# Hymba decoder step: the memory projection interleaved with the two norms around it

## The reference, cut to what matters

```
mk, mv = mem @ w_xk, mem @ w_xv                     # memory keys and values, both are outputs
h = h + rms_norm(merged @ w_out, n_mix_post)        # output projection, its norm, the residual
xn = rms_norm(h, n_x_pre)                           # norm ahead of the cross-attention
q = xn @ w_xq                                       # query projection
def rms_norm(x, g): return x * rsqrt(mean(x * x, -1) + 1e-6) * g
```

## Time and profile before

| | us |
|---|---|
| median of 3 runs | 1958.95 (1956.95 to 1961.89) |
| profiled execution | 1959.56 |
| its span | 1958.0 |
| TensorE busy in it | 1809.5 (92%) |
| VectorE, ScalarE, GpSimd busy | 949.1, 500.0, 117.1 |

### The profile page before, as it was taken

How to read it: one execution, slowest core, us unless ns; L and a number is a source line. 1 busy time by engine, 2 the same in 40 slices (tenths; PEclk the granted TensorE clock), 3 DMA queues, 4 the chain that set the end, 5 groups by cost and what they waited for, 6 DMA issues and landing times.

```text
span 1958.0 us, 32059 instructions
## 1 busy us (share of the span) xinstructions
PE 1809.5 (92%) x12999; PEld 1653.0 (84%) x12999; DVE 949.1 (48%) x1145; ACT 500.0 (26%) x862; POOL 117.1 (6%) x145
## 2 busy tenths in 40 slices
PE   7999989989989968998999699999999999999993
PEld 6999976555568957896789579999999999999982
DVE  6328888776655286422342583333233332233445
ACT  6212125666464112203331231110001000000122
POOL 2100020001320010001100110000000000000000
PEclk9999999999999989998999899999999999999995
DMA  5512137657883114114311121111112111111113
GB/s 168 147 56 76 54 122 216 200 165 213 305 260 132 43 65 172 65 43 151 121 52 43 43 108 45 43 43 44 43 43 58 49 43 44 43 43 37 49 55 122
DMA packets 136958, 187.28 MB, mean 96 GB/s; under 512 B 7705, under 2 KB 99035, under 8 KB 136344
## 3 DMA queue, kind: packets, MB, share of 16 engines
q1 hardware_dynamic: 122670, 121.47, 20.4%
q0 software_dynamic: 14192, 64.53, 9.3%
q10 hardware_dynamic: 2, 0.00, 0.0%
HBM read 165.65 MB, written 20.74 MB: 95 GB/s over the span
## 4 chain that ended last, share of the span: by engine, by line
PE 84%; DVE 6%; ACT 6%; issue 3%; DMA 0%; SPq 0%; DVEq 0%; POOLq 0%; ACTq 0%; POOL 0%
PE PS L1712 20%; PE PS L1713 20%; PE PS L1714 20%; PE PS L1702 7%; PE PS L1919 2%; PE PS L1941 2%; PE PS L1965 2%; PE PS L1840 2%; PE PS L2210 2%; ACT KTS L729 1%; PE PS L2002 1%; PE PS L1727 1%; PE PS L2231 1%; DVE Y L1232 1%; PE PS L1728 1%
## 5 line engine op out<-in xcount | busy, mean ns | idle before, releaser
L1712 PE MATMUL PS<-XH,WH 128*128 128x352 f32 x1968 | 635.6, 323 | 0.0
L1713 PE MATMUL PS<-XL,WH 128*128 128x352 f32 x1968 | 630.8, 321 | 0.0
L1714 PE MATMUL PS<-XH,WL 128*128 128x352 f32 x1968 | 630.5, 320 | 0.0
L1132 DVE CAST WH<-RAW 128x1024 fp32r<-128x1024 f32 x126 | 95.3, 757 | 690.2 <-PE PS L1714 667.3
L1713 PEld LDWEIGHTS PS<-XL,WH 128*128 128x128 f32 x1968 | 369.8, 188 | 0.0
L1712 PEld LDWEIGHTS PS<-XH,WH 128*128 128x128 f32 x1968 | 369.2, 188 | 0.0
L1714 PEld LDWEIGHTS PS<-XH,WL 128*128 128x128 f32 x1968 | 368.9, 187 | 0.0
L1273 DVE SCALAR_TENSOR_TENSOR CY<-GP,DW,CY 128x1024 f32<-128x1024 f32 x124 | 158.5, 1278 | 1.0 <-DVE CY L1276 1.0
L1134 DVE TENSOR_TENSOR WL<-RAW,WH 128x1024 fp32r<-128x1024 f32 x126 | 156.5, 1242 | 4.3
L1712 PE MATMUL PS<-HH,WH 128*128 128x352 f32 x462 | 149.0, 323 | 0.0
L1713 PE MATMUL PS<-HL,WH 128*128 128x352 f32 x462 | 148.1, 321 | 0.0
(11 more groups left out here) (339 smaller groups left out, 2326.0 us busy)
## 6 DMA issues: line engine op xcount, KB each, us to landing
PG<-in_cache_k SPq DMA_DIRECT2D x128, 256.0 KB, 3.0
PG<-in_cache_v SPq DMA_DIRECT2D x64, 256.0 KB, 4.2
PG<-in_cache_v POOLq DMA_DIRECT2D x64, 256.0 KB, 4.4
RAW<-in_w_gate SPq DMA_DIRECT2D x22, 512.0 KB, 4.0
RAW<-in_w_up SPq DMA_DIRECT2D x22, 512.0 KB, 5.1
RAW<-in_w_in SPq DMA_DIRECT2D x20, 512.0 KB, 6.4
h_spill<-H POOLq DMA_DIRECT2D x2, 4224.0 KB, 12.2
H<-h_spill POOLq DMA_DIRECT2D x2, 4224.0 KB, 13.5
```

The source lines that it names most:

```text
L1132: dve.tensor_copy(WH[v % 2][:, :, :], raw).then_inc(hi_done, 1)
L1712: pe.matmul(out, WH[u][:, k, :], xh[:, k, cols], start=(k == 0), stop=False)
L1713: pe.matmul(out, WH[u][:, k, :], xl[:, k, cols], start=False, stop=False)
L1714: mm = pe.matmul(out, WL[u][:, k, :], xh[:, k, cols], start=False, stop=(k == kt - 1))
```

## The change

- The transposes of the memory move in between output tiles 3 to 6, two channel tiles after each. MH and ML move to another place in memory, since the output projection still reads the old one. The memory's load is issued ahead of H's.
- The roots are taken "in columns": the sum over channels of 88 tokens is one matmul with the tokens as the weights and one column of ones moving, so 12 such matmuls leave 1056 sums in 88 partitions by 12 columns (`token_sums`). Root and reciprocal work on those 12 columns. Four matmuls a chunk spread them again over all partitions (`spread`). Both norms do so; the second one's sums and spread stand inside the first two query tiles.
- The memory's high weight parts are copied by ScalarE (`high_at`), VectorE makes the low parts (`low_at`). Key tiles, sums, spread and the work of the norms alternate in a written-out order.
- A value tile takes the memory as weights and the 128 weight columns as the moving operand, twice, for the two halves of the memory tokens (`mem_value_tile`). The result has tokens on partitions, so values are not turned back.
- H gets Y added on VectorE for even k and on GpSimd for odd k; the squares of H, now in Y, are added up in TB by GpSimd, one of eight adds for each k.
- Stores and loads on GpSimd's queue wait for the new semaphores in their places.

The diff, cut (the same names with unchanged meaning left out):

```diff
@@ memory
-        MH = at("MH", [P, KT, NMEM], F32R, R1)
-        ML = at("ML", [P, KT, NMEM], F32R, R1 + 8192)
-        VMT = at("VMT", [P, KT, NMEM], F32, R1 + 16384)
-        KMTOK = at("KMTOK", [P, 2, D], F32, R1 + 24576)
+        MH = at("MH", [P, KT, NMEM], F32R, R2B + 16384)
+        ML = at("ML", [P, KT, NMEM], F32R, R2B + 24576)
+        KMTOK = at("KMTOK", [P, 2, D], F32, R2B + 16384)
...
+        W88, N88 = 88, T // 88
+        YRT, HRT = SMALL[0:W88, 96:96 + N88], SMALL[0:W88, 108:108 + N88]
@@ gpsimd
+            pool.wait_ge(h_back, 16)
+            pool.wait_ge(y_summed, 1)
+            steps = 0
+            for k in range(KT):
+                if k % 2:
+                    pool.wait_ge(y_scaled, k + 1)
+                    pool.tensor_tensor(H[:, k, :], H[:, k, :], Y[:, k, :], ALU.add).then_inc(h_new, 1)
+                    steps += 1
+                pool.wait_ge(h_squared, k + 1)
+                if k:
+                    pool.wait_ge(h_new, steps)
+                    pool.tensor_tensor(TB[:, :], TB[:, :], Y[:, k, :], ALU.add).then_inc(h_new, 1)
+                else:
+                    pool.tensor_copy(TB[:, :], Y[:, k, :]).then_inc(h_new, 1)
+                steps += 1
...
-            pool.wait_ge(h_summed, KT * n_x + KT)
+            pool.wait_ge(mem_k_out, 16)
             for n in range(2):
                 memory_in(n)
@@ scalar
+            def high_at(t):
...
+                act.wait_ge(tile_done, t + 1)
+                copy(WH[t % 2][:, :, :], RAW[t // 2 % 2][:, :, P * (t % 2):P * (t % 2) + P]).then_inc(hi_done, 1)
...
+                if 3 <= n < 7:
+                    mem_high(2 * n - 6)
+                    mem_high(2 * n - 5)
+                if n == 6:
+                    high_at(MEM)
+            high_at(MEM + 1)
+            act.wait_ge(y_summed, 1)
+            root(YRT, PS[0:W88, 7, 0:N88], y_root, eps=EPS[0:W88, :])
+            for t in range(2):
+                high_at(MEM + t + 2)
+                mem_taken(t)
+            for k in range(KT):
+                if k % 2:
+                    act.wait_ge(h_new, 3 * (k // 2) + 2)
+                else:
+                    act.wait_ge(h_new_v, k // 2 + 1)
+                act.activation(Y[:, k, :], H[:, k, :], ACT.Square).then_inc(h_squared, 1)
+                act.activation(XH[:, k, :], H[:, k, :], ACT.Identity, scale=vec("x_pre", k)).then_inc(in_hi, 1)
+                for t in (2 * k + 2, 2 * k + 3):
+                    if t + 2 < 2 * KT:
+                        high_at(MEM + t + 2)
+                    if t < 2 * KT:
+                        mem_taken(t)
+            for a in range(2):
+                mem_rows_taken(a)
@@ vector
+            dve.wait_ge(y_root, 1)
+            dve.reciprocal(YRT, YRT).then_inc(inverse, 1)
+            low_at(MEM + 2)
+            low_at(MEM + 3)
...
+            for k in range(KT):
+                dve.scalar_tensor_tensor(out=tok3(Y[:, k, :]), in0=tok3(Y[:, k, :]), scalar=vec("mix_post", k),
+                                         in1=PS[:, 4:7, 0:CHUNK], op0=ALU.mult, op1=ALU.mult).then_inc(y_scaled, 1)
+                if k % 2 == 0:
+                    dve.wait_ge(y_scaled, k + 1)
+                    dve.tensor_tensor(H[:, k, :], H[:, k, :], Y[:, k, :], ALU.add).then_inc(h_new_v, 1)
+                for t in (2 * k + 4, 2 * k + 5):
+                    if t < 2 * KT:
+                        low_at(MEM + t)
+                if k:
+                    x_low_part(k - 1)
+                if k >= KT - 2:
+                    split_at(MEM, 3, k - 2)
+            x_low_part(KT - 1)
@@ tensor
+            def token_sums(src, col):
+                for b in range(N88):
+                    x = pe.matmul(PS[0:W88, 7, col + b:col + b + 1], src[:, W88 * b:W88 * b + W88], ONES[:, 0:1],
...
+            def spread(r, c, bank):
+                for j in range(4):
+                    x = pe.matmul(PS[:, bank, W88 * j:W88 * j + W88],
+                                  r[:, 4 * c + j:4 * c + j + 1].to_broadcast([W88, P]), IDENT[0:W88, 0:W88],
...
+            def mem_value_tile(j):
...
+                for a in range(2):
+                    out = PS[:, 3 * u, P * a:P * a + P]
+                    keys = slice(P * a, P * a + P)
+                    for k in range(KT):
+                        pe.matmul(out, MH[:, k, keys], WH[u][:, k, :], start=(k == 0), stop=False)
+                        pe.matmul(out, MH[:, k, keys], WL[u][:, k, :], start=False, stop=False)
+                        x = pe.matmul(out, ML[:, k, keys], WH[u][:, k, :], start=False, stop=(k == KT - 1))
...
+            for t in range(KT):
+                tile(MEM + t, t % 2, MH, ML, chunks=1, width=NMEM)
+                if t == 1:
+                    pe.wait_ge(y_added, YN["out"] + KT)
+                    pe.wait_ge(psum_free, MEM + AHEAD)
+                    token_sums(TB, 0).then_inc(y_summed, 1)
+                if t == 2:
+                    pe.wait_ge(inverse, INVERSES["mix_post"])
+                    for c in range(3):
+                        x = spread(YRT, c, 4 + c)
+                    x.then_inc(y_summed, 1)
+            for j in range(KT):
+                mem_value_tile(j)
+            mem_rows(0)
+            pe.wait_ge(y_scaled, KT)
+            mem_rows(1)
...
+            pe.wait_ge(memkv_taken, 1)
+            first_tile(t1, XH, XL, input_of("x"))
+            pe.wait_ge(h_new, KT + KT // 2)
+            token_sums(TB, 400).then_inc(h_summed, 1)
...
+            tile(t1 + 1, 1, XH, XL, between=root_spread)
```

More of the change, by code:

```diff
@@ L1027, in _, with mem_high @@
+            def mem_high(k):
                 act.wait_ge(mem_turned, k + 1)
                 copy(MH[:, k, :], PS[:, 6 + k % 2, 0:NMEM]).then_inc(mem_hi, 1)
[L1029 to L1046, removed]
+            def mem_taken(t):
+                act.wait_ge(tile_done, MEM + t + 1 + AHEAD)
+                src = PS[:, 3 * (t % 2), 0:NMEM]
+                if t < KT:
+                    copy(KMT[:, t, :], src).then_inc(psum_free, 1)
+                else:
+                    copy(VM[:, :, P * (t - KT):P * (t - KT) + P], src.rearrange("p (a d) -> p a d", a=2))\
+                        .then_inc(psum_free, 1)
@@ L1544, in _ @@
                     .then_inc(mem_lo, 1)
[L1546 to L1551, removed]
+            dve.memset(TB[:, :], 0.0).then_inc(squares_zero, 1)
+            dve.wait_ge(squares_zero, 1)
+            for n in range(KT):
+                if n < KT - 2:
+                    split_at(TILE0["out"], n // 4, n % 4 + 2)
+                else:
+                    low_at(TILE0["out"] + n + 2)
+                dve.wait_ge(y_squared, n + 1)
+                dve.wait_ge(y_added, n)
+                dve.tensor_tensor(TB[:, :], TB[:, :], TA[:, :], ALU.add).then_inc(y_added, 1)
+                if 3 <= n < 7:
+                    mem_low(2 * n - 6)
+                    mem_low(2 * n - 5)
@@ L1714, in tile @@
                         mm = pe.matmul(out, WL[u][:, k, :], xh[:, k, cols], start=False, stop=(k == kt - 1))
+                    if between is not None and c < chunks - 1:
+                        between(c)
                 mm.then_inc(tile_done, 1)
@@ L2171, in _, with mem_turn @@
             tile(t1 + 1, 1, XH, XL)
-            with pe.Fori(1, PAIRS["out"]) as i:
-                for u in range(2):
-                    tile(t1 + 2 * i + u, u, XH, XL)
-            def post_norm(norm, name):
-                pe.wait_ge(y_added, YN[name] + KT)
-                sum_over_channels(0, TB, True, True).then_inc(y_summed, 1)
-            pe.wait_ge(mem_in, 16)
-            for k in range(KT):
+            def mem_turn(k):
+                pe.wait_ge(mem_in, 16)
                 if k >= 2:
@@ new lines, in _, with post_norm @@
+            for n in range(2, KT):
+                tile(t1 + n, n % 2, XH, XL)
+                if 3 <= n < 7:
+                    mem_turn(2 * n - 6)
+                    mem_turn(2 * n - 5)
+            def post_norm(norm, name):
+                pe.wait_ge(y_added, YN[name] + KT)
+                sum_over_channels(0, TB, True, True).then_inc(y_summed, 1)
+            def mem_value_tile(j):
+                t, u = MEM + KT + j, j % 2
+                pe.wait_ge(split_done, t + 1 + AHEAD_RAW)
+                pe.wait_ge(psum_free, t + 1)
+                for a in range(2):
[5 more added lines that the diff above has]
+                        x = pe.matmul(out, ML[:, k, keys], WH[u][:, k, :], start=False, stop=(k == KT - 1))
+                x.then_inc(tile_done, 1)
@@ L2206, in cross_scores @@
+            pe.wait_ge(memkv_taken, 2)
+            tile(t1 + 1, 1, XH, XL, between=root_spread)
+            with pe.Fori(1, PAIRS["xq"]) as i:
+                for u in range(2):
+                    tile(t1 + 2 * i + u, u, XH, XL)
             def cross_scores(q, h):
```

108 lines of the change are left out of this document (67 added, 41 removed).

## The result

The changed kernel takes 1988.01 us (median of 4 runs, 1987.02 to 1991.65) where the kernel before took 1959.69 beside it: a ratio of 1.0141, 95% interval 1.0122 to 1.0161. It is 28 us slower, and the prediction of no change was wrong. The profiled execution took 1991.65 us.

The account below looks back on a forecast made before the run. Between output and query projection, TensorE waits on splits, norms and vector work, 107.7 us. Terms 1.8 + 100 + 6.6 = 108.4, so +0.7 us: forecast 1960 us, range 1949 to 1975.

Parts of the forecast that it names:

- (1): Memory's turns between output tiles 3 to 6: 0.46 us each four, 1.8 us added; 7.6 us leave the later stretch.
- (2): From the last output tile's end (T) through key tiles, sums, root and spread: first scaling of Y starts at 20 us.
- (3): Eight serial rounds of vector-engine work, one per channel tile: 8.2, then 10.8 odd, 9.6 even; value tile 0 at 46.4.
- (4): Unturned value tiles: 48 passes of 128 columns, 0.113 us each, 5.4 us a tile; value tile 5 ends at 80.6.
- rival C: Value passes: load hidden, a pass takes 0.068 us, rounds bind; -4.5 us, 1956; chance 0.05.
- one term, 1.7 us: In the value tiles: 1.7 us added for a half-clock start after the gap before them.
- Rival B: Value tiles: clock falls in about half the time because half the cycles move nothing; +10 to +14, 1972; chance 0.06.
- Rival A: Value passes lose their rate at 128 columns, 0.222 us each, 10.7 us a tile; +36, 1996; chance 0.10.
- (5): Tail from value tile 5's end to first query matmul: 19.8 us less overlaps 0.4, reaching 100 us after T.
- (6): Query projection: second sums 1.9, spread 2.7 and first tile at half clock 2 us; 6.6 us longer.
- Sum: Whole change: 1.8 + 100 + 6.6 = 108.4 against 107.7, +0.7 us; bounds some -10 to +9.
- The clearest gain: First norm: reciprocal over 1056 columns cost 6.76 us; on few columns taken for as little as the root's 0.29.

Follow-up runs that it names:

- The kernel with the high copies first: Changed kernel with values turned again, plus ScalarE making a round's two high copies ahead of its square and scaling: 1943.88 us, ratio 0.9910.
- the one without GpSimd: Kernel with values turned and ScalarE's high copies ahead of the square, GpSimd's additions moved to VectorE: 1939.19 us, ratio 0.9880.
- the extra passes: Changed kernel with 96 extra passes of 256 memory columns between the last key tile and the first value tile: 1974.05 us in one execution.
- twice the columns: Changed kernel, each value pass streaming its 128 weight columns twice, the second copy thrown away: 1963.55 us, ratio 1.0003 to the kernel before.
- the kernel where they stood behind a gap: Kernel with GpSimd's additions on VectorE, token sums and spread each one key tile earlier: 1935.17 us, ratio 0.9876.

## Why the prediction was wrong, step by step

(1) **Turns in the output projection**: right. Four transposes take the place of 0.36 to 0.45 us at 645.63, 657.67, 669.57 and 681.60, as the 0.46 each. T itself cannot show the 1.8: it stands 5.3 us later than before, and 2.5 of that lie ahead of the output projection, whose first pass starts at 591.87 against 589.36.

(2) **To the first scaling**: right. Tile 1 at T + 4.5 (4.5), 24 sum passes 0.076 apart, TensorE idle to T + 12.0 (12.3), key tile 2 at half clock up to its last passes (4.96 us), 24 spread passes 0.11 apart, first scaling at T + 20.01 (20).

(3) **Rounds**: right. 8.1, 10.9 and 9.6 us (8.2, 10.8, 9.6); value tile 0 at T + 46.4 (46.4). The first four scalings, one a round, from VectorE's rows of the changed kernel in order of time:

```profile
713.51 1.31 DVE L1627 SCALAR_TENSOR_TENSOR Y<-Y,VECS,PS 128x1056 f32<-128x1056 f32 x1 [6.84 <-PE PS L2283]
...
721.64 1.31 DVE L1627 SCALAR_TENSOR_TENSOR Y<-Y,VECS,PS 128x1056 f32<-128x1056 f32 x1
...
732.50 1.30 DVE L1627 SCALAR_TENSOR_TENSOR Y<-Y,VECS,PS 128x1056 f32<-128x1056 f32 x1
...
742.12 1.30 DVE L1627 SCALAR_TENSOR_TENSOR Y<-Y,VECS,PS 128x1056 f32<-128x1056 f32 x1
```

The kernel with the high copies first shows that they were serial, and the one without GpSimd that the holds cost more than the additions would on VectorE. From round 3 on the value tiles at half clock set the pace: 20.5 us a round.

(4) **Value passes**: this step failed. At full clock a pass takes 0.112 us, as the step took it from the load rows (0.113), so rival C is out. The Trainium skill's page "TensorE: Matmul & The Clock Gate", section "Back-to-back issue gap", gives about 81 ns; no stretch of these passes is faster than 112 ns. But the step put the passes at full clock, with one term, 1.7 us, for a half-clock start after the gap. That term measured 37.7: eight tiles took 80.9 us where 8 x 5.4 is 43.2, and the end of the last stands at T + 127.3. Rival B named the right quantity, the clock, and had it wrong in size and in cause: half clock was to hold for half of the time, and held for 79.77 of 80.9 us; and it was to fall because half of the cycles move nothing, while the same passes ran 32.6 us at 1.00 behind the extra passes. B had 0.06, for the reason "TensorE has no gaps there"; the gap that preceded the fall lies ahead of the stage, and step (3) had it: TensorE idle in each of the first rounds. Rival A's price, 0.222 a pass, came near the 0.213 measured by luck, since its cause, a rate of the format, is out. What the step took for granted is that a stream without gaps brings the clock back, as it does in the 256-column rows, and no row of that kind had 128 columns. Part 1 of the same page of the Trainium skill says that "activity releases the throttle". Here TensorE worked without a gap for 79.77 us at 0.50, so this stream did not release it, and the measurement decides.

(5) **Tail**: not put to the test in the changed kernel, where the slow value tiles left the other engines 3.6 us of work. With twice the columns the query projection starts at T + 101.7, against 100.

(6) **Query projection**: 5.3 us longer (6.6); its first tile met a gap of only 0.65 us and ran at a clock of 1.00, so the 2 us of half clock did not come. With twice the columns they did, and more: 99.5 us against 91.5.

**Sum**: with the clock up, in the kernel with twice the columns, the change costs nothing measurable (1.0003), which agrees with the sum of +0.7 us. With the clock down the query projection begins at T + 131 and not near T + 100 or 102, and the kernel is 28 us slower.

**The clearest gain** of step (2), the short root and reciprocal, is one on VectorE, and no gain by itself: alone it moved nothing.

What stays open: why the clock came back under passes of 256 columns and not under those of 128 (the runs changed the columns, and nothing else about them), and what makes a gap count. Ahead of the falls within 128-column passes TensorE had gaps of 1.3 to 2.4 us in four kernels; one of 0.5 us in front of such passes was followed by no fall. But length alone does not decide. In the kernel before, the gap ahead of the same value tile 0 was as long as in the changed kernel (2.14 against 2.12 us idle), and its 256-column passes stayed at 1.00:

```profile
741.71 0.38 PE L1712 MATMUL PS<-MH,WH 128*128 128x256 f32 x1 [2.14 <-DVE WL L1134]
...
741.71:746.00 4.29, 3.13 (x24) 2.92 (x24) 4.22 (x5) 0.38 (x1) 0.00 (x0) 1.00 0.00 0
```

An earlier gap there of the same idle time (2.16 us, to 722.46) was followed by half clock. So a gap preceded every fall in the value tiles, but the runs don't establish that a gap by itself brings the clock down.

## What to carry to other kernels

In a stage of narrow matmul passes look at the granted clock: here it paid to enter it at full clock and keep it free of gaps, or to make the passes wider. The same loads with twice the columns, half of them thrown away, took the value tiles from 10.2 to 5.8 us. When a long operation of one engine is shortened, look first at what ran under it. Where two engines take turns, move to the front of the turn what the other waits for; and an addition given to GpSimd to spare VectorE can cost VectorE more than it saves (3.51 us in place of 1.31 for one held operation, against 1.25 for the addition).

## What was not expected of the hardware

The granted clock kept the level that it had: the same stream of 128-column passes ran 32.6 us at 1.00 when it came from full clock without a long gap, and 79.77 us at 0.50 once the clock had fallen behind one. In these four kernels the fall came late, 0.9 to 2.4 us after TensorE was at work again. And loads follow the clock too: 24 passes of one moving column, nothing but loads, are 0.076 us apart at full clock and 0.148 in the kernel where they stood behind a gap.
